# Where the causal mask of the prompt attention is added: TensorE's identity product or VectorE's addition in PSUM

## What is computed

```python
s = jnp.einsum('bqhd,bshd->bhqs', qb, k).astype(jnp.float32) * scale + cb[..., :, None] - c[..., None, :]
qpos = start + jnp.arange(Q_BLOCK)
p = _masked_softmax(s, (kpos[None, :] <= qpos[:, None])[None, None])
return jnp.einsum('bhqs,bshd->bqhd', p.astype(v.dtype), v)
```

## Time and profile before

| | us |
|---|---|
| median of three runs | 1977.03 |
| lowest, highest | 1970.47, 1977.34 |
| the profiled execution, in all | 1972.52 |
| its span in the trace | 1970.7 |
| TensorE matmul busy, of the span | 1507.9 (77%) |
| VectorE busy | 735.8 (37%) |
| ScalarE busy | 222.7 (11%) |
| mean granted TensorE clock, of full speed | 0.817 |

### The profile page before, as it was taken

How to read it: one execution, slowest core, us unless ns; L and a number is a source line. 1 busy time by engine, 2 the same in 40 slices (tenths; PEclk the granted TensorE clock), 3 DMA queues, 4 the chain that set the end, 5 groups by cost and what they waited for, 6 DMA issues and landing times. The chain is left out here.

```text
span 1970.7 us, 26263 instructions
## 1 busy us (share of the span) xinstructions
PE 1507.9 (77%) x8356; PEld 1060.6 (54%) x8356; DVE 735.8 (37%) x1188; ACT 222.7 (11%) x609; POOL 229.9 (12%) x157
## 2 busy tenths in 40 slices
PE   0666636999978799884457776866867989999997
PEld 0666635878767655552322432422432868888852
DVE  2343212100033335665776667667650110101012
ACT  0000022010010023441000000000000000000012
POOL 0000000100030000004054144135130000000000
PEclk9988877999985568997567667667667999999999
DMA  8764032122232140004897898798764262222200
GB/s 227 208 174 143 27 128 76 45 65 65 65 89 44 22 183 1 1 1 135 284 332 255 272 329 273 253 324 284 245 228 138 80 203 70 68 76 69 58 11 33
DMA packets 212965, 275.05 MB, mean 140 GB/s; under 512 B 37629, under 2 KB 136470, under 8 KB 212430
## 3 DMA queue, kind: packets, MB, share of 16 engines
q1 hardware_dynamic: 151118, 172.18, 27.9%
q10 hardware_dynamic: 55328, 83.91, 13.4%
q0 software_dynamic: 6432, 17.83, 2.7%
HBM read 266.93 MB, written 11.11 MB: 141 GB/s over the span
## 5 line engine op out<-in xcount | busy, mean ns | idle before, releaser
L1440 POOL DMA_INDIRECT d_slc<-in_cache_nsa_slc,selrow x128 | 196.6, 1536 | 342.6 <-PE bank L1529 300.7
L1464 PE MATMUL bank<-d_vpage,d_pf 128*8 128x512 f32 x512 | 178.2, 845 | 57.0 <-DMA d_vpage<-in_cache_fox_kv 56.3
L223 PE MATMUL score_banks<-c_cols,c_w 64*64 64x128 f32 (+1 forms) x2048 | 122.0, 281 | 115.5 <-DVE c_cols L259 115.5
L579 PE MATMUL score_banks<-xnT,p_w 128*128 128x260 f32 (+2 forms) x896 | 201.5, 385 | 10.1 <-DMA p_w<-in_w_in 10.1
L579 PEld LDWEIGHTS score_banks<-xnT,p_w 128*128 128x128 f32 (+2 forms) x896 | 164.6, 185 | 42.3 <-DMA p_w<-in_w_in 10.3
L223 PEld LDWEIGHTS score_banks<-c_cols,c_w 64*64 64x64 f32 x2048 | 121.2, 141 | 116.2 <-issue 116.2
L1609 DVE TENSOR_TENSOR d_product<-d_kpage,d_qrow 128x2048 f32<-128x2048 f32 x64 | 146.0, 2291 | 69.5 <-DMA d_kpage<-in_cache_fox_kv 65.6
L1615 DVE TENSOR_REDUCE d_sf<-d_product 128x32 f32<-128x2048 f32 x64 | 145.8, 2278 | 0.0
L1853 PE MATMUL score_banks<-xnT,e_wg 128*128 128x260 f32 x512 | 117.6, 389 | 15.7 <-DMA e_wb<-in_w_branch 9.0
L1853 PEld LDWEIGHTS score_banks<-xnT,e_wg 128*128 128x128 f32 x512 | 98.1, 193 | 33.9 <-DVE e_tmp L1879 9.5
L1464 PEld LDWEIGHTS bank<-d_vpage,d_pf 128*8 128x8 f32 x512 | 17.9, 100 | 182.6 <-DMA d_vpage<-in_cache_fox_kv 140.2
(11 more groups left out here) (331 smaller groups left out, 1764.4 us busy)
## 6 DMA issues: line engine op xcount, KB each, us to landing
d_kpage<-in_cache_fox_kv SPq DMA_DIRECT2D x256, 256.0 KB, 10.2
d_vpage<-in_cache_fox_kv ACTq DMA_DIRECT2D x256, 256.0 KB, 3.6
c_page<-in_cache_nsa_cmp ACTq DMA_DIRECT2D x128, 128.0 KB, 3.0
c_page<-in_cache_nsa_cmp SPq DMA_DIRECT2D x128, 128.0 KB, 3.1
p_w<-in_w_in SPq DMA_DIRECT2D x13, 1024.0 KB, 5.3
e_wg<-in_w_in SPq DMA_DIRECT2D x24, 512.0 KB, 4.2
d_mem<-in_cache_mem_kv SPq DMA_DIRECT2D x16, 512.0 KB, 9.0
e_w<-in_w_in SPq DMA_DIRECT2D x6, 1024.0 KB, 5.4
```

Source lines behind the costliest of these rows:

```text
L223: last = nc.tensor.matmul(hp[s][half][rows, v, 0:n], w1[rows, v, d, :], cols[s][rows, v, d, 0:n], start=d == 0, stop=d == HD - 1)
L579: last = nc.tensor.matmul(pj[ch.n % 2][i][0:ch.w, 0:NM if ch.mem else TH], w[:, c, ch.off:ch.off + ch.w], rhs, start=c == 0, stop=c == DC - 1)
L1440: nc.gpsimd.indirect_dma_start(out=slc[:, n, :], out_offset=None, in_=k.cache_slc, in_offset=bass.IndirectOffsetOnAxis(ap=k.selrow[:, at:a ...
L1464: last = nc.tensor.matmul(fv_bank[part:part + H, :], pf[:, page, :], vpage[:, slot, :], start=page < 4, stop=page >= PAGES - 4)
```

## The change

In `scores` the identity products are gone: the last product of a fox unit is now that of the gates, and in the sparse units the query-key product is the last. In `maximum`, VectorE first adds the mask to the diagonal 128 columns of both banks in one instruction, in place in PSUM, raises a new semaphore `masked`, waits for it, and then reduces as before. Nothing else moves.

```diff
--- before.py
+++ after.py
@@ -1187,6 +1187,7 @@
             sem("f_" + n) for n in ("s_done", "m_done", "e_done", "rc_done", "gr_done", "p_done", "turned"))
         pt_left, pt_right, o_done, out_done = (sem("f_" + n) for n in ("pt_left", "pt_right", "o_done", "out_done"))
         o_out = [sem(f"f_o_out{i}") for i in range(2)]
+        masked = sem("f_masked")
         score = lambda u: [ps[2 * (u.no % 2)], ps[2 * (u.no % 2) + 1]]
         both = lambda u: k.score_banks[:, 2 * (u.no % 2):2 * (u.no % 2) + 2, 0:u.n]
         pt_bank, o_bank = ps[4:6], ps[6:8]
@@ -1216,18 +1217,14 @@
                 def scores(u):
                     if u.no >= 2:
                         te.wait_ge(e_done, 2 * (u.no - 1))
-                    more = u.kind != "mem"
+                    more = u.kind == "fox"
                     for j in range(2):
                         last = nc.tensor.matmul(score(u)[j][:, 0:u.n], query(u, j), key(u, j), start=True, stop=not more,
                                                 skip_group_check=True)
-                    if u.kind == "fox":
-                        for j in range(2):
-                            nc.tensor.matmul(score(u)[j][:, 0:u.n], k.ident[0:H, 2 * u.c + j:2 * u.c + j + 1].to_broadcast([H, P]),
-                                             k.ncum[:, 0:u.n], start=False, stop=False, skip_group_check=True)
                     if more:
                         for j in range(2):
-                            last = nc.tensor.matmul(score(u)[j][:, u.t * P:u.n], k.ident, k.causal, start=False, stop=True,
-                                                    skip_group_check=True)
+                            last = nc.tensor.matmul(score(u)[j][:, 0:u.n], k.ident[0:H, 2 * u.c + j:2 * u.c + j + 1].to_broadcast([H, P]),
+                                                    k.ncum[:, 0:u.n], start=False, stop=True, skip_group_check=True)
                     last.then_inc(s_done, 1)
 
                 def turn(u):
@@ -1275,6 +1272,10 @@
             def _(ve):
                 def maximum(u):
                     ve.wait_ge(s_done, u.no + 1)
+                    if u.kind != "mem":
+                        own = both(u)[:, :, u.t * P:u.n]
+                        nc.vector.tensor_tensor(own, own, k.causal.unsqueeze(1).to_broadcast([P, 2, P]), ALU.add).then_inc(masked, 1)
+                        ve.wait_ge(masked, sum(v.kind != "mem" for v in units[:u.no + 1]))
                     nc.vector.tensor_reduce(nm[:, u.no, :], both(u), AX, ALU.max, negate=True).then_inc(m_done, 1)
 
                 def normalise(u):
```

## The result

The changed kernel took 1975.65 us in the median of 22 runs, the kernel before 1970.47 us in 22 runs beside it; the ratio is 1.0027, with a 95% interval of 1.0018 to 1.0036. So the move of the mask costs some 5 us, less than the 0.5% that was set as the bound of "the same", but beyond its own scatter. The profiled execution of after took 1975.43 us, with a span of 1973.6 (1970.7 before); that is 2.9 us more than the profiled execution of before (1972.52), which itself lay 2.0 us above the median of its kernel.

A forecast was written before the change was run, and what follows sets the result against it. TensorE looked like the bound, with waits in a ring through VectorE. The terms -4.4 - 4.0 + 0.3 = -8.1 us, plus 10.4 for the clock, gave +2.3 and a forecast of 1978.0 us, range 1965 to 1989.

The forecast's parts named there:

- The addition: On VectorE, 48 mask additions over 128x256 elements with the result in PSUM, 0.42 us each.
- rival C: The addition into PSUM costs its upper bound, 0.27 us more each, +7.3, about 1985 us; 7 in 100.
- Start: First 27 us, at half clock: five mask pairs leave TensorE's queue, against a new wait of 0.67; -4.4 us.
- Forgetting rounds at full clock: Three rounds of the forgetting attention: 1.32 us shorter each, -4.0 us in all at unchanged clock.
- the ring: Scores, maximum, exponential, placing and transposing: 0.18 us shorter per unit where VectorE is free, 0.50 instead of 0.68.
- Sparse rounds at full clock: Eight rounds of the sparse branch: +0.04 us each when placed in order; +0.3 us taken for all.
- The clock: Across the prompt attention stage, lost TensorE work means more half-clock time: +10.4 us, bounds 0 to +25.
- the first two parts: Clock rise no sooner than 718.8, 5 us later on average (+1.8, +2.0); later forgetting rounds ten more at half (+4.0).
- The third part: Sparse rounds: seven clock dips in eight rounds, not five, +2.6 us.
- A: The clock keeps its pattern, so the full gain of -8.1 us stays, about 1969 us; 18 in 100.
- B: The clock is chronically lower in the forgetting attention and every sparse round: +14.4 us, about 1991 us; 10 in 100.
- D: TensorE's reprieve shortens the copies' waits too, below 1967 us; 5 in 100.

The follow-up runs named there:

- the two halves: The changed kernel with VectorE adding the mask only in the forgetting attention (1.0021) or only in the sparse units (0.9988), TensorE keeping the others.
- e12: The kernel before with unused filling products and the gates' product over 128 rows instead of 8; ratio to before 0.9883.
- e9: The changed kernel with unused filling products and the gates' product over 128 rows instead of 8; ratio to before 0.9847, 1942.42 us.
- e11: The changed kernel with the gates' product over 128 rows instead of 8, no filling products; ratio to before 0.9897.
- e10: The kernel before with the gates' product over 128 rows instead of 8, nothing else; ratio to before 0.9906.
- e5: The changed kernel with one unused full-array product on TensorE in each of twelve masked sets; ratio to before 0.9931, 1955.28 us.
- e7_thin: Against e1_both, TensorE's identity product replaced by one of 8 rows and equal columns that adds zeros; ratio to before 1.027, 2023.0 us.
- e1_both: The changed kernel with TensorE's identity products kept, so both engines add the mask; ratio to before 1.007.
- e4_sparse_only: The changed kernel with VectorE adding the mask in the 32 sparse units only, TensorE in the forgetting attention; ratio to before 0.9988.

## Why the prediction was right, and where it wasn't

*The whole.* I gave 1978.0 and "the same"; measured are 1975.65 and +0.27%. In the profile the stage grew by 0.9 us where my sum had 2.3. The timed runs say 5.2. Of the other 4.3, 2.0 lie outside the stage in the two profiled executions (the sample stage, above all), and 2.3 in that before's profiled execution was 2.0 slower and after's 0.2 faster than the median of its kernel. Which of this the change causes is open: the timed ratios of the two halves (1.0021 and 0.9988) add up to 1.0009 +/- 0.0015, less than 1.0027 (1.0018 to 1.0036), though the two intervals overlap. That the same instructions took 76.0 or 79.9 us in two executions is large enough for it; that it explains it is not shown.

*The median of before* that I started from, 1977.03 of three runs, was high: 22 runs gave 1970.47. My 1978.0 stands for a base of 1975.7 and a loss of 2.3, so the base was 5.2 us too high and the loss 2.9 too low. That the forecast lay 2.4 us from the result is partly luck.

*The addition* was to take 0.42 us and took 0.43, so rival C had no ground. (Its own sum, 9.6, also lay below the 9.9 that it was said to pass.) The idle before t2 was to be 2.6 us in a sparse round (2.59), and TensorE was to wait anew for a copy before t3 (0.55).

*Start:* -4.4 expected. The stretch up to the first t2 transposes went from 23.95 to 19.45 us, -4.5, with the new wait of 0.67 in its place:

```profile
710.40 1.51 PE L1237 MATMUL bank<-cst 128*128 128x128 f32 x6 [0.67 <-DVE f_pt L1296]
```

*Forgetting rounds at full clock:* -1.32 each expected. After had none at full clock. With wide gates they are 15.84 us (e12) and 14.97 (e9, e11): **-0.87**. The term was too large. The pair of masks at t1' and that at t2' were worth 0.44 us each, not 0.5 and 0.64, since a mask product behind a wide one is cheaper; and the 0.18 on the ring from the scores of t3 to the transposes of t2 didn't come (6.61 us in e10, 6.62 in e11), because there the mask pair delayed the maximum by no more than the addition does. With 8-row gates no profile has both kernels at full clock, so for them the term isn't measured.

*Sparse rounds at full clock:* +0.04 each expected. Rounds of 12.09 and 13.07 us became 12.12 and 13.10 (e5, e9): +0.03. Most of the gain of 0.18 on the ring is there (4.88 us from the scores of t3 to the transposes of t2 before, 808.58 to 813.46, and 4.72 in e5_fill, 831.86 to 836.58), and VectorE's queue takes it back.

*The clock:* the direction was right and it ate the gain, as forecast. The amount and the price were both off, in opposite senses. I expected some 22 us more at half clock, it was 37.9. In the first two parts I was near. Between the first t2 transposes and the rise of the clock there were 7.8 us at half instead of 2.9, though the rise itself came at 718.2 us, as before (718.7), and not 5 us later. In the forgetting rounds after it there were 24.7 instead of 13.6, eleven more where I had ten. The third part, the dips of the sparse rounds, was the one mis-sized: I had two dips more (6.8 us), it was 26.5 us more, since every sparse round fell to half clock, mostly for 4.0 or 6.2 us.

The price held in the forgetting rounds and not in the sparse ones. The three forgetting rounds together took 59.8 us (55.9 before). With -0.87 each at equal clock the clock cost 6.5 us there, 0.41 for each of 16.0 more at half. In the sparse rounds it cost hardly 1.3 us for the 26.5, because most of it fell into waits: against eight rounds at full clock (4 x 12.12 + 4 x 13.10 = 100.9) after's 109.8 are 8.9 us for 43.6, 0.20 for each, while before's five dips cost 7.7 us for 17.1, 0.45 for each. So by these estimates the clock cost 7.8 us and not 10.4, and the gain at equal clock was 6.9 and not 8.1. That far more dips came than I counted, at a far lower price each, is luck: their share was to be 2.6 us and was about 1.3.

*What caused it* I had half right. I wrote that the mask products were "among the fullest work of the low stretches"; e7_thin shows that their rows count. The Trainium skill ("TensorE: Matmul & The Clock Gate", "A second HAM failure mode: psum-queue depth-cycling") puts the loss down to small idle times of the engine between its groups of products. e1_both has longer ones than before (2.08 against 1.61 us) and in the profile nearly the same clock (0.86 against 0.87); e7_thin has less idle time than e1_both in the stage (24 against 29 us) and the lowest clock of all (0.69). Idle time may have its share in the sparse rounds of after; e5_fill, in which three of the eight rounds dip, doesn't separate it, since it shortens the gap and adds work on the whole array at once.

*The rivals.* A (clock unchanged, -8 us) didn't come; e12 against e9 shows 3.3 us for the same move with the clock near full. B (chronic, +14) didn't come as a time, though its dips did: every sparse round fell, at hardly any price. D didn't.

## What to carry to other kernels

Before taking "useless" products off TensorE, look at the granted clock around them: where other work there uses few rows or leaves gaps, a product over the whole array may pay for itself by the clock. Where the clock sits at half although TensorE is busy, look for products with few rows; filling the rows with zeros cost nothing that these profiles show and won 0.9%. And judge an effect of a few microseconds by repeated runs, since one profile shows one pattern of the clock out of several; the mean clock of each timed run tells whether the profile is typical.

## What the runs showed of the hardware that I had not expected

- 8 rows against 128 in products of equal columns and number: 163.5 against 61.0 us at half clock, and 41.7 us more for the stage (e7_thin, e1_both). Without any product in that place it was 95.5 (after).
- A 128-row product takes as long as an 8-row one: 1.98 us for the four of 512 columns in both, and the next 128-row pair starts 0.09 us sooner behind it (1.82 us after its start, not 1.91).
- One filler of 0.9 us in each of twelve sets, unused, is worth 20 us to the changed kernel (1975.65 to 1955.28; the runs of before beside each had medians of 1970.47 and 1970.24).
- In after the sparse rounds fell into step with the clock: 14.41 and 12.90 us by turns, three times over, with 6.2 and 4.0 us at half in each. The last rounds of e4_sparse_only and e11_wide_after do the same (about 14.5 and 12.9).
